# Two-block transformer on one core: the norms' logarithm and exponential from one table set, pair sums on VectorE, low halves by tile, fewer filler matmuls

## The chip, the cores and the metric

The kernel runs on one core of a Trainium2 chip. The metric is the device time of one launch in microseconds, taken as the median over runs. The engines are TensorE (PE), VectorE (DVE), ScalarE (ACT), GpSimd (POOL), and SyncE (SP), which issues the weight transfers.

## The reference: what is computed

Two stacks of two layers each, over 256 tokens of width 1024. In the first, every layer is three half steps, and each ends in the same update: a layer norm of a weighted sum of the input and a gated branch. The result goes, scaled and shifted, into the next matrix product. The second stack, over 272 rows, normalises by the root mean square (RMS) ahead of a mixer with three branches and of a gated convolutional feed-forward.

```python
def layer_norm(x, g, b):
    mu = jnp.mean(xf, axis=-1, keepdims=True)
    var = jnp.mean(jnp.square(xf - mu), axis=-1, keepdims=True)
    return ((xf - mu) * lax.rsqrt(var + LN_EPS)) * g + b
def post_norm_update(x, y, gate, res_w, g, b):
    return layer_norm(DN_ALPHA * x + res_w * gate * y, g, b)
def _rms(x):
    return xf * lax.rsqrt(jnp.mean(xf * xf, axis=-1, keepdims=True) + EPS)
# mixer: retention, hgrn2 and differential attention, each head's output
# through _rms, then a gate, then a product with w_branch
```

There are six layer norms (0 to 5) and five RMS norms of the whole width (0 to 4; the last is the output). The three mixers of each layer have an RMS norm over each head.

## The kernel before

Activations lie feature-major: a tile `k` (0 to 7) holds 128 features on the partitions and the tokens along the free axis, 512 tokens in norms 0 (latent and context rows), 256 in norms 1 to 5, 272 in the RMS norms. Every matrix product is done in three passes on numbers split into a high and a low half: `high*high`, `high*low`, `low*high`. Weights come in chunks of four tiles: SP loads `raw`, ACT casts it to `high` (L2068), DVE subtracts to get `low` (L2291). With `NSLOT` = 4 slots these run up to four chunks ahead of TensorE. The order of work on each engine is the order in which the code of its block issues it; engines meet only in semaphores. A *unit* is 256 output columns: two chunks of four input tiles each (in the steps after a norm), and in each chunk `j` = 0 and 1 pick the output tile, so that every input tile is used in a chunk with `j` = 0 and again with `j` = 1.

A norm is a place where the next product needs the norm's result and TensorE has nothing else to do. For a layer norm the chain is: ones-matmuls sum the rows; DVE centres them in four pairs of tiles (`TC`, L2597); ACT squares each pair (`TQ`, L2233); TensorE sums the eight squared tiles with eight ones-matmuls (L547), two behind each pair; ACT takes the logarithm (L2235) and the exponential (L2238), which is `rdev`, the reciprocal deviation. Then, tile by tile, DVE scales (`scaled`, L2335), ACT adds the shift and casts to the high half (L2082), and DVE subtracts for the low half (`x_low_pair`, L2345). TensorE waits for low halves in pairs of tiles (`s_xl`), in the first unit. The RMS norms do the same with `rms_act` (L1735, L1738) and `rms_dve` (L1749, L1754), the latter in halves of four tiles.

ScalarE keeps one set of function tables at a time. The builder puts an `ACT_TABLE_LOAD` ahead of a function that the loaded set lacks: in every norm one ahead of the logarithm and another ahead of the exponential. The sigmoids need a third set.

`keep_busy(pe, n)` issues `n` matmuls whose result nobody reads (L553), to fill TensorE's time in the chain: three after the row sums, four ahead of the wait for `rdev` and six behind it.

At the end of a mixer of the second stack the heads' outputs are squared, summed on TensorE, and go through logarithm and exponential (`tail_logs`, L711 and L715; `tail_exps`, L724), in two halves, on ScalarE; DVE scales, ACT and DVE split into `OH` and `OL`. Meanwhile TensorE works at the merge gates (`mgate`) from weights split early (`early_split`). Ahead of the `branch` product TensorE waits for a bank that the sigmoid of a merge gate (L2154) must have read; DVE passes that on (L2500). In mixer 1 TensorE also waits, ahead of the merge gates, for the first logarithm (`s_oln`).

## Time and profile before

| | |
|---|---|
| Device time, median of 3 runs | 3049.11 us (3046.49 to 3050.3) |
| Span of the profiled execution, first to last instruction | 3044.0 us |
| TensorE busy with matmuls, fillers among them | 2923.9 us (96%) |
| VectorE busy | 1757.0 us (58%) |
| ScalarE busy | 1380.5 us (45%) |
| Mean granted clock of TensorE, share of full | 0.991 |

The profile gives for its own execution the span; a device time is given for the runs alone, and their median lies 5.1 us above the span, which is what is around it. TensorE's busy time counts fillers too, so 96% overstates what it does for the result. In rows of the timeline a float32 matmul of the ones has two records, so that "x16" is eight matmuls.

### The profile page before, as it was taken

To read this page: it belongs to the slowest core of one execution; us is meant where nothing else is said; L and a number is where in the kernel's file an instruction comes from. 1 tells how busy PE (TensorE), PEld (TensorE's weight loads), DVE (VectorE), ACT (ScalarE), POOL (GpSimd) and SP (SyncE) were. 2 spreads that over 40 slices of the span, in tenths; PEclk is the share of its full clock that TensorE was granted. 3 is DMA by queue.
4 is the path that set the end of the run, shared out by engine and by line. 5 is a ranking of instruction groups with operands and counts; after the bars stand their busy time and mean duration, and the time that the engine had idled before them with its cause. 6 is when DMAs were issued, how large, how long until landed. Compare 5 with 4: busy or idle time off the path is not lost. (4 is left out here: it accounts for less than half of the span.)

```text
span 3044.0 us, 51451 instructions
## 1 busy us (share of the span) xinstructions
PE 2923.9 (96%) x19512; PEld 2567.3 (84%) x19512; DVE 1757.0 (58%) x2624; ACT 1380.5 (45%) x1948; POOL 375.6 (12%) x306
## 2 busy tenths in 40 slices
PE   6999999899999999999899999999999999999998
PEld 3667766677888889888899889799999998988998
DVE  2323224266766657665545865757745577566784
ACT  1222213135655545554453553556644454546663
POOL 2111000123111110111100110101101002020110
PEclk9999999999999999999999999999999999999999
DMA  9886353741565655465435405245545451533563
GB/s 331 281 253 189 114 160 127 194 152 56 165 186 147 193 183 152 147 192 184 133 121 170 146 30 179 84 144 147 170 158 158 142 163 44 156 108 115 156 179 132
DMA packets 586156, 474.80 MB, mean 156 GB/s; under 512 B 28720, under 2 KB 547888, under 8 KB 585664
## 3 DMA queue, kind: packets, MB, share of 16 engines
q1 hardware_dynamic: 584464, 460.44, 49.3%
q0 software_dynamic: 1520, 11.95, 1.3%
q8 instruction: 122, 2.00, 0.3%
q14 instruction: 50, 0.41, 0.0%
HBM read 471.23 MB, written 4.72 MB: 156 GB/s over the span
## 5 line engine op out<-in xcount | busy, mean ns | idle before, releaser
L2291 DVE TENSOR_TENSOR low<-raw,high 128x1024 fp32r<-128x1024 f32 (+1 forms) x744 | 905.6, 1220 | 811.7 <-ACT high L2068 809.3
L2068 ACT CAST high<-raw 128x1024 fp32r<-128x1024 f32 (+1 forms) x744 | 768.3, 1034 | 1001.6 <-PE PS L1980 600.6
L1978 PE MATMUL PS<-NHh,high 128*128 128x272 f32 (+1 forms) x2304 | 669.2, 290 | 14.2 <-DVE NHl L1754 4.7
L1980 PE MATMUL PS<-NHh,low 128*128 128x272 f32 (+1 forms) x2304 | 661.2, 287 | 0.0
L1979 PE MATMUL PS<-NHl,high 128*128 128x272 f32 (+1 forms) x2304 | 660.2, 287 | 0.0
L1978 PEld LDWEIGHTS PS<-NHh,high 128*128 128x128 f32 x2304 | 433.4, 188 | 19.5 <-issue 15.4
L1979 PEld LDWEIGHTS PS<-NHl,high 128*128 128x128 f32 x2304 | 434.0, 188 | 0.8
L1980 PEld LDWEIGHTS PS<-NHh,low 128*128 128x128 f32 x2304 | 433.7, 188 | 0.0
L1976 PE MATMUL PS<-XX,high 128*128 128x512 f32 x966 | 346.8, 398 | 0.0
L1978 PE MATMUL PS<-XX,high 128*128 128x512 f32 (+1 forms) x752 | 273.6, 364 | 3.7 <-DVE XX L2345 2.2
L1975 PE MATMUL PS<-XX,low 128*128 128x256 f32 x966 | 271.2, 281 | 0.3
L1979 PE MATMUL PS<-XX,high 128*128 128x512 f32 (+1 forms) x752 | 266.0, 354 | 0.0
L1980 PE MATMUL PS<-XX,low 128*128 128x512 f32 (+1 forms) x752 | 265.8, 354 | 0.0
L1976 PEld LDWEIGHTS PS<-XX,high 128*128 128x128 f32 x966 | 181.5, 188 | 37.6
L1978 PEld LDWEIGHTS PS<-XX,high 128*128 128x128 f32 x752 | 143.5, 191 | 54.6 <-issue 35.5
L1975 PEld LDWEIGHTS PS<-XX,low 128*128 128x128 f32 x966 | 182.3, 189 | 8.0 <-issue 1.1
L2673 POOL TENSOR_TENSOR GG<-SG,GG 128x256 f32 (+1 forms) x92 | 94.1, 1023 | 729.6 <-ACT GG L2187 639.9
L1980 PEld LDWEIGHTS PS<-XX,low 128*128 128x128 f32 x752 | 143.4, 191 | 20.3
L1979 PEld LDWEIGHTS PS<-XX,high 128*128 128x128 f32 x752 | 143.6, 191 | 17.8
L1976 PE MATMUL PS<-GG,high 128*128 128x512 f32 x420 | 149.4, 398 | 0.0
L1975 PE MATMUL PS<-GG,low 128*128 128x256 f32 x420 | 118.1, 281 | 0.9 <-POOL GG L2673 0.9
L1978 PE MATMUL PS<-OH,high 128*128 128x272 f32 (+1 forms) x384 | 111.7, 291 | 4.6 <-DVEq L2500 4.6
(355 smaller groups left out, 4938.9 us busy)
## 6 DMA issues: line engine op xcount, KB each, us to landing
raw<-w_in_dram SPq DMA_DIRECT2D x416, 256.0 KB, 3.1
raw<-ffn_w_in_dram SPq DMA_DIRECT2D x352, 256.0 KB, 3.4
part<-ada_w_dram SPq DMA_DIRECT2D x184, 256.0 KB, 4.2
raw<-w_ffn_in_dram SPq DMA_DIRECT2D x176, 256.0 KB, 3.2
raw<-ffn_w_out_dram SPq DMA_DIRECT2D x160, 256.0 KB, 3.1
raw<-w_branch_dram SPq DMA_DIRECT2D x96, 256.0 KB, 3.1
raw<-w_ffn_out_dram SPq DMA_DIRECT2D x80, 256.0 KB, 2.9
part_sg<-ada_w_dram SPq DMA_DIRECT2D x48, 256.0 KB, 3.0
```

The lines of the kernel that those rows point to most:

```text
L1975: nc.tensor.matmul(out, wl, xh, start=False, stop=False)
L1976: last = nc.tensor.matmul(two, wh, both, start=False, stop=end)
L1978: nc.tensor.matmul(out, wh, xh, start=begin, stop=False)
L1979: nc.tensor.matmul(out, wh, xl, start=False, stop=False)
L1980: last = nc.tensor.matmul(out, wl, xh, start=False, stop=end)
L2068: nc.scalar.copy(high[:, slot, 0:nk, :], raw[:, slot, 0:nk, :]).then_inc(s_high, 1)
L2291: nc.vector.tensor_tensor(low[:, slot, 0:nk, :], raw[:, slot, 0:nk, :], high[:, slot, 0:nk, :].bitcast(F32), ALU.subtract).then_inc(s_low, 1)
L2673: nc.gpsimd.tensor_tensor(out, x, h.bitcast(F32), ALU.subtract).then_inc(s_hl, 1)
```

## The change

1. **One set.** `log_exp_set()` asks for the set that holds both logarithm and exponential. It is called at the start of every step `res` and `add` (the residual products ahead of the norms), at the start of mixer 0's end, in mixer 1's end behind the early gates, and ahead of mixer 2's small exponential. The sigmoids behind each norm load their own set as before.
2. **Squares in pairs.** For the last two pairs of squared tiles DVE adds the two tiles of the pair (`s_sqp`), and TensorE sums the result with one ones-matmul instead of two: six in place of eight. Only in the layer norms.
3. **Vectors earlier.** The per-feature vectors of a norm (`columns`, `xg`, `xb`) are made in the residual step behind its second unit (`norm_vectors`), no longer between centring and `rdev`.
4. **By tile.** DVE's `scaled` and low-half operations are interleaved, two tiles apart, and TensorE waits tile by tile. In the RMS norms the low halves are made in pairs of tiles in place of fours, and TensorE waits by pairs.
5. **Fewer fillers.** Four and six around the wait for `rdev` become two and three; in the RMS norms five and five become two and four.

```diff
-        def ret_act(act, layer, early_split, early_gate):
+        def ret_act(act, layer, early_split, early_gate, log_exp_set):
+            log_exp_set()
...
             early_gate(1)
+            log_exp_set()
             early_split(1)
...
             dve.wait_ge(s_rrd, m + 1)
-            for hf in range(2):
-                for k in range(4 * hf, 4 * hf + 4):
-                    out = s_rmod if m < 4 else s_modd_final
-                    nc.vector.scalar_tensor_tensor(TN[:, k, :], H[:, k, :], col(name, layer * KT + k),
-                                                   RS[:, 1, 0:T2], ALU.mult, ALU.mult).then_inc(out, 1)
-                if m < 4:
-                    k = slice(4 * hf, 4 * hf + 4)
-                    dve.wait_ge(s_rxh, 4 * m + 2 * hf + 2)
-                    nc.vector.tensor_tensor(NHl[:, k, :], TN[:, k, :], NHh[:, k, :].bitcast(F32),
-                                            ALU.subtract).then_inc(s_rxl, 1)
+            def low_pair(v):
+                k = slice(2 * v, 2 * v + 2)
+                dve.wait_ge(s_rxh, 4 * m + v + 1)
+                nc.vector.tensor_tensor(NHl[:, k, :], TN[:, k, :], NHh[:, k, :].bitcast(F32),
+                                        ALU.subtract).then_inc(s_rxl, 1)
+
+            for k in range(KT):
+                out = s_rmod if m < 4 else s_modd_final
+                nc.vector.scalar_tensor_tensor(TN[:, k, :], H[:, k, :], col(name, layer * KT + k),
+                                               RS[:, 1, 0:T2], ALU.mult, ALU.mult).then_inc(out, 1)
+                if m < 4 and k >= 2 and k % 2 == 0:
+                    low_pair(k // 2 - 1)
+            if m < 4:
...
-                                if name in ("glu", "v", "cgate") and (rolled(s) or not u) and j == 0 and k % 2 == 0:
-                                    pe.wait_ge(s_xl, 4 * norms + (k0 + k) // 2 + 1)
+                                if name in ("glu", "v", "cgate") and (rolled(s) or not u) and j == 0:
+                                    pe.wait_ge(s_xl, KT * norms + k0 + k + 1)
+                                if s.get("after_rms") and (rolled(s) or not u) and j == 0 and k % 2 == 0:
+                                    pe.wait_ge(s_rxl, 4 * (rmss - 1) + (k0 + k) // 2 + 1)
...
-                    for v in range(4):
+                    for v in range(2):
                         pe.wait_ge(s_sq, 4 * norms + v + 1)
-                        last = ones_pair(VAR_BANK, TQ, T, v)
+                        ones_pair(VAR_BANK, TQ, T, v)
+                    for v in (2, 3):
+                        pe.wait_ge(s_sqp, 2 * norms + v - 1)
+                        last = nc.tensor.matmul(PS[:, VAR_BANK, 0:T], ones[:], TQ[:, 2 * v, 0:T], start=False,
+                                                stop=(v == 3))
                     last.then_inc(s_var, 1)
                     norms += 1
-                    keep_busy(pe, 4)
+                    keep_busy(pe, 2)
                     pe.wait_ge(s_rdev, norms)
-                    keep_busy(pe, 6)
+                    keep_busy(pe, 3)
                     if norms == 6:
                         for v in range(4):
                             rms_pe_pair(pe, rmss, v)
                         rmss += 1
-                        keep_busy(pe, 5)
+                        keep_busy(pe, 2)
                         pe.wait_ge(s_rrd, rmss)
-                        keep_busy(pe, 5)
+                        keep_busy(pe, 4)
                 if s.get("rms"):
                     pe.wait_ge(s_free, U_end + 2)
                     keep_busy(pe, 2)
                     rms_pe_pair(pe, rmss, 3)
                     rmss += 1
                     if rmss < 5:
-                        keep_busy(pe, 5)
...
+            def log_exp_set():
+
+                nc.scalar.preload_act_table_set("natural_log_exp_and_others")
...
+                if name in ("res", "add"):
+                    log_exp_set()
...
                     if s.get("at") == 9216 and u == 2:
+                        log_exp_set()
                         lambda_act(act, s["layer"])
...
+            def norm_vectors(m):
+
+                if m < 5:
+                    dve.wait_ge(s_mod, (6 * (m + 1) + 3) // TURN + 1)
+                    columns(m + 1)
+                al = ALPHA if m < 5 else 1.0
+                link(nc.vector.tensor_scalar(sm("xg"), col("ln_g", m * KT, KT), al, None, ALU.mult))
+                link(nc.vector.tensor_scalar(sm("xb"), col("ln_b", m * KT, KT), al, None, ALU.mult))
...
+                    if name == "res" and u == 1:
+                        norm_vectors(norms)
...
+                    for v in (2, 3):
+                        dve.wait_ge(s_sq, 4 * m + v + 1)
+                        nc.vector.tensor_tensor(TQ[:, 2 * v, 0:T], TQ[:, 2 * v, 0:T], TQ[:, 2 * v + 1, 0:T],
+                                                ALU.add).then_inc(s_sqp, 1)
                     if m < 5:
                         dve.wait_ge(s_mod, (6 * (m + 1) + 5) // TURN + 1)
-                        columns(m + 1)
                         gates(m + 1)
-                    al = ALPHA if m < 5 else 1.0
-                    link(nc.vector.tensor_scalar(sm("xg"), col("ln_g", m * KT, KT), al, None, ALU.mult))
-                    link(nc.vector.tensor_scalar(sm("xb"), col("ln_b", m * KT, KT), al, None, ALU.mult))
...
-                        for hf in range(2):
-                            scaled(hf, T)
-                            x_low_pair(m + 1, 2 * hf, T)
-                            x_low_pair(m + 1, 2 * hf + 1, T)
+                        scaled(0, T)
+                        scaled(1, T)
+                        for k in range(KT):
+                            if k + 2 < KT:
```

How the order moves, at three places. The first is ScalarE around norm 1 (`TQ` are squares, `RS` the deviation, `XX` the high halves). Before:

```order
L2068 CAST high<-raw 128x1024 x8
L2233 ACTIVATE TQ<-TC 128x2x256 x4
L2235 ACT_TABLE_LOAD
L2235 ACTIVATE RS<-PS,epsc 128x256
L2238 ACT_TABLE_LOAD
L2238 ACTIVATE RS<-RS 128x256
L2082 ACTIVATE XX<-TQ,small 128x256 x8
```

and now:

```order
L2108 ACT_TABLE_LOAD
L2079 CAST high<-raw 128x1024 x8
L2250 ACTIVATE TQ<-TC 128x2x256 x4
L2252 ACTIVATE RS<-PS,epsc 128x256
L2255 ACTIVATE RS<-RS 128x256
L2093 ACTIVATE XX<-TQ,small 128x256 x8
```

The two loads within the norm are gone, and one stands ahead of the eight casts of the residual step's weights. The second place is VectorE in the same norm (`TC` centred rows, `small` the per-feature vectors, `XX` the low halves). Before:

```order
L2597 SCALAR_TENSOR_TENSOR TC<-PS,X 128x2x256 x4
L2306 TENSOR_SCALAR small<-mod 128x8
L2307 TENSOR_TENSOR small<-small,cols 128x8
L2308 TENSOR_TENSOR small<-small,mod 128x8
L2309 TENSOR_TENSOR small<-small,cols 128x8
L2313 TENSOR_SCALAR small<-mod 128x8
L2604 TENSOR_SCALAR small<-cols 128x8
L2605 TENSOR_SCALAR small<-cols 128x8
L2335 SCALAR_TENSOR_TENSOR TQ<-TC,small,RS 128x256 x4
L2345 SCALAR_TENSOR_TENSOR XX<-TQ,small,XX 128x256 x4
L2335 SCALAR_TENSOR_TENSOR TQ<-TC,small,RS 128x256 x4
L2345 SCALAR_TENSOR_TENSOR XX<-TQ,small,XX 128x256 x4
```

and now:

```order
L2624 SCALAR_TENSOR_TENSOR TC<-PS,X 128x2x256 x4
L2628 TENSOR_TENSOR TQ<-TQ 128x256 x2
L2340 TENSOR_SCALAR small<-mod 128x8
L2361 SCALAR_TENSOR_TENSOR TQ<-TC,small,RS 128x256 x3
L2370 SCALAR_TENSOR_TENSOR XX<-TQ,small,XX 128x256
L2361 SCALAR_TENSOR_TENSOR TQ<-TC,small,RS 128x256
L2370 SCALAR_TENSOR_TENSOR XX<-TQ,small,XX 128x256
L2361 SCALAR_TENSOR_TENSOR TQ<-TC,small,RS 128x256
L2370 SCALAR_TENSOR_TENSOR XX<-TQ,small,XX 128x256
```

Six small operations have left the norm (they stand in the residual step, behind its second unit), two additions of squares have come in, and the groups of four scalings and four low halves have become a run in which they take turns. The third is ScalarE at the end of mixer 1 (`QB` squares of the heads, `MJ` logarithm and exponential, `GR_108` gates). Before:

```order
L2123 ACTIVATE GR_108<-PS 128x544
L2068 CAST high<-raw 128x1024
L1312 ACTIVATE QB<-PS 128x544 x4
L711 ACT_TABLE_LOAD
L711 ACTIVATE MJ<-PS,epsc 128x1088
L2068 CAST high<-raw 128x1024
L711 ACTIVATE MJ<-PS,epsc 128x1088
L724 ACT_TABLE_LOAD
L724 ACTIVATE MJ<-MJ 128x1088 x2
```

and now:

```order
L2137 ACTIVATE GR_108<-PS 128x544
L2108 ACT_TABLE_LOAD
L2079 CAST high<-raw 128x1024
L1315 ACTIVATE QB<-PS 128x544 x4
L712 ACTIVATE MJ<-PS,epsc 128x1088
L2079 CAST high<-raw 128x1024
L712 ACTIVATE MJ<-PS,epsc 128x1088
L725 ACTIVATE MJ<-MJ 128x1088 x2
```

Of the two loads one has gone, and the other stands ahead of the cast and the squares.

## Rows read from the trace of the kernel before

**Rows 1.** page, its first line and busy time of TensorE

```profile
span 3044.0 us, 51451 instructions
...
PE 2923.9 (96%) x19512; PEld 2567.3 (84%) x19512; DVE 1757.0 (58%) x2624; ACT 1380.5 (45%) x1948; POOL 375.6 (12%) x306
```

**Rows 2.** chain of waits, TensorE: who waited for whom, us, times, longest

```profile
PE PS L1978 <- DVEq L2500: 4.6, 2, 2.5
```

**Rows 3.** groups by line, ScalarE: busy us, mean ns | idle before

```profile
L2238 ACT ACT_TABLE_LOAD x6 | 7.7, 1283 | 0.1
...
L1738 ACT ACT_TABLE_LOAD x5 | 6.4, 1283 | 0.1
```

**Rows 4.** timeline of norm 1: start, us, engine, line, operation, count, [idle before <-releaser]

```profile
753.71 2.42 ACT L2233 ACTIVATE TQ<-TC 128x512 f32<-128x512 f32 x4 [1.89 <-DVE TC L2597]
...
754.39 3.72 PE L547 MATMUL PS<-TQ,ones 128*128 128x256 f32 x16 [0.32 <-ACT TQ L2233]
...
758.15 0.47 ACT L2235 ACTIVATE RS<-PS,epsc 128x256 f32<-128x256 f32 x1 [0.72 <-PE PS L547]
...
758.64 1.28 ACT L2238 ACT_TABLE_LOAD   x1
...
759.93 0.42 ACT L2238 ACTIVATE RS<-RS 128x256 f32<-128x256 f32 x1
...
760.40 2.46 PEld L553 LDWEIGHTS PS<-con,ones 128*128 128x128 f32 x12 [0.97 <-ACT RS L2238]
...
760.49 1.67 DVE L2335 SCALAR_TENSOR_TENSOR TQ<-TC,small,RS 128x256 f32<-128x256 f32 x4 [3.73 <-ACT RS L2238]
...
763.10 0.47 PE L1972 MATMUL PS<-XX,high 128*128 128x512 f32 x1
...
765.25 1.67 DVE L2345 SCALAR_TENSOR_TENSOR XX<-TQ,small,XX 128x256 fp32r<-128x256 f32 x4
```

**Rows 5.** timeline, one VectorE addition-sized operation

```profile
775.32 0.43 DVE L2539 TENSOR_TENSOR SG<-SG,GU 128x256 f32<-128x256 f32 x1 [0.50 <-ACT SG L2184]
```

**Rows 6.** timeline of norm 0 (two rows)

```profile
498.33 7.10 PE L547 MATMUL PS<-TQ,ones 128*128 128x512 f32 x16 [1.20 <-ACT TQ L2233]
...
513.23 0.47 PE L1978 MATMUL PS<-XX,high 128*128 128x512 f32 x1 [2.22 <-DVE XX L2345]
```

**Rows 7.** timeline of the second RMS norm

```profile
2059.16 0.65 ACT L1742 CAST NHh<-TN 128x544 fp32r<-128x544 f32 x1 [0.98 <-DVE TN L1749]
...
2058.21 1.74 DVE L1749 SCALAR_TENSOR_TENSOR TN<-H,cols,RS 128x272 f32<-128x272 f32 x4 [3.22 <-ACT RS L1738]
...
2064.32 1.29 DVE L1754 TENSOR_TENSOR NHl<-TN,NHh 128x1088 fp32r<-128x1088 f32 x1 [0.71 <-ACT NHh L1742]
...
2065.75 0.36 PE L1978 MATMUL PS<-NHh,high 128*128 128x272 f32 x1 [0.29 <-DVE NHl L1754]
```

**Rows 8.** timeline, end of mixer 1 of layer 0

```profile
1808.80 1.28 ACT L711 ACT_TABLE_LOAD   x1
...
1811.31 0.39 PE L1978 MATMUL PS<-NHh,high 128*128 128x272 f32 x1 [1.11 <-ACT MJ L711]
...
1813.28 1.28 ACT L724 ACT_TABLE_LOAD   x1
...
1825.77 0.57 PE L1978 MATMUL PS<-OH,high 128*128 128x272 f32 x1 [2.10 <-DVEq L2500]
```

**Rows 9.** windows: busy us of each engine, then clock, DMA share, GB/s

```profile
510.00:513.00 3.00, 1.01 (x5) 0.56 (x3) 3.00 (x9) 2.46 (x7) 0.00 (x0) 1.00 0.00 0
...
1471.60:1475.00 3.40, 3.38 (x8) 2.54 (x9) 0.00 (x0) 2.89 (x4) 0.00 (x0) 0.50 0.00 0
...
1475.00:1478.40 3.40, 3.40 (x11) 2.64 (x10) 0.00 (x0) 0.00 (x0) 0.00 (x0) 0.64 0.00 0
...
1825.80:1828.00 2.20, 2.20 (x10) 2.20 (x11) 1.50 (x2) 2.20 (x4) 0.00 (x0) 0.50 0.69 236
...
1828.00:1831.00 3.00, 3.00 (x22) 3.00 (x22) 2.09 (x2) 1.29 (x2) 0.00 (x0) 0.83 0.52 163
```

More of the change, by code:

```diff
@@ L1288, in level_exps, with hg_act @@
             nc.scalar.activation(er, er, ACT.Exp).then_inc(s_ha, 1)
-        def hg_act(act, layer, early_split, early_gate, early_logits):
+        def hg_act(act, layer, early_split, early_gate, log_exp_set, early_logits):
             t, d, a, p = HT * layer, HDV * layer, HAC * layer, HPO * layer
@@ L2083, in x_high_pairs @@
                                                     bias=sm("ab", c)[:, k:k + 1])
-                    if k % 2:
-                        last.then_inc(s_xh, 1)
+                    last.then_inc(s_xh, 1)
             def residual_rows(m, T):
@@ L2263, in _ @@
                                                           lambda u: early_sigmoid(u, steps[n_step + 1]),
-                                                          *([lambda: early_logits(steps[n_step + 1])]
-                                                            if s["mixer"] == 1 else []))
+                                                          *(([log_exp_set], [log_exp_set,
+                                                                             lambda: early_logits(steps[n_step + 1])],
+                                                             [])[s["mixer"]]))
                 if name == "branch" and s["n"] == 2:
```

53 lines of the change are left out of this document (27 added, 26 removed).

## The prediction, made before the run

> **What bounds the kernel now.** The page gives a span of 3044.0 us with TensorE busy for 96% of it [rows 1]. Fillers count as busy, so the places where TensorE does nothing for the result have to be found in the timeline, at each norm. In norm 1 [rows 4] the four pairs of tiles are squared from 753.71 to 756.13; TensorE sums them from 754.39 for 3.72 us without a gap behind its start, so its eight matmuls and not ScalarE end that stage. Then everything is one chain: logarithm at 758.15, a table load at 758.64, exponential at 759.93, VectorE's scaling at 760.49, and TensorE takes up the product at 763.10. The six fillers (2.86 us from 760.40) are about as long as the stop behind the exponential, so they fill it and lengthen it by 0.1 us at most. Such a stop comes 11 times (six layer norms, five RMS norms), and whatever shortens its chain shortens the span by as much, provided that TensorE is not held by the fillers. The groups by line say that the second load stands in each: 6 and 5 times 1283 ns with nearly no idle time ahead [rows 3]. The chain of waits then shows one more place: twice, 4.6 us in all, TensorE waits for VectorE's release of a bank ahead of a branch product [rows 2], and its timeline [rows 8] shows two table loads in the ScalarE work that leads there.
>
> **The change, part by part.**
>
> *Loads.* From the load's start to the exponential's is 1.29 us in norm 1 [rows 4]; the chain has nothing beside it there. 11 x 1.29 = **14.2 us**. The first load of each norm (ahead of the logarithm) lies behind the squares while TensorE still sums, so removing it gives nothing. The load now at the start of `res` and `add` steps lands on ScalarE, busy 45% of the span [rows 1], with weights split up to four chunks ahead: nothing; uncovered it would be 1.28 each.
>
> The Trainium skill ("ScalarE: Activation LUTs", What ACT_TABLE_LOAD costs) puts about 1.38 us of drain on top of the load, 2.66 us for a switch. The trace doesn't show that: the logarithm ends at 758.62, the load begins at 758.64, the exponential 1.29 us behind it [rows 4]. By the page the sum would be some 15 us larger.
>
> *Squares in pairs.* Eight matmuls take 3.72 us in norm 1, 0.465 each, and 7.10 in norm 0, 0.89 each [rows 4, 6]. Two fewer: 1.8 us in norm 0, 0.93 in norms 1 to 5, 4.65 together. Now VectorE must have the last sum in time: square at 756.13, an addition of 128x256 takes 0.43 [rows 5], so 756.6, and TensorE comes to its sixth matmul at 754.39 + 5 x 0.465 = 756.7. It fits with 0.1 to spare; without it I would lose some tenths a norm. I take **6.4 us**. The vectors that leave the norm ended long ahead of the exponential, so their move gives nothing there, but it makes room for the additions. In the residual step six to ten small operations of VectorE (58% busy) now stand ahead of a low half; I take nothing, with 1 us for each of six norms at the far end.
>
> *Waits by tile, layer norms.* VectorE does 16 operations from 760.49 to 766.92 [rows 4], 0.40 apart. Before, tiles 0 and 1 are there at +2.4 and TensorE starts at 763.10, +2.6. Now tile 0 comes after four operations, +1.7, then one more tile per 0.8 us, and tile 7 at the same +6.4. But a tile's three passes need 0.36 us, so TensorE waits between tiles, ends the first chunk's second output tile at about +5.9 and the second chunk at +8.7, just where it ends before (the last low half, then 2 x 0.36 and 4 x 0.36). An earlier start is spent waiting: **0**, between -0.8 (the whole earlier start) and +0.2 a norm.
>
> *RMS norms.* Before [rows 7]: scalings from 2058.21, the second half's low operation ends at 2065.61, TensorE's second chunk starts at 2065.75, +7.5. It needs 3.05 us: +10.6. Now pairs: scalings at 0.43, a cast of 0.65 and a low operation of half of 1.29 plus fixed cost, say 0.7; in turn they give pairs at +2.4, 4.3, 6.1 and 8.0. TensorE then has one pair with `j` = 0 (0.76) and the whole of `j` = 1 (1.52) left: +10.3. Saves 0.3, four times: **1.2 us**.
>
> *Fillers.* They hide nothing for the result, but if they were left at four and six, they would now be late: the six summing matmuls end at 757.2, two fillers of 0.48 end at 758.1, and `rdev` comes at about 758.2; four would hold TensorE until 759.1. Behind it three end at +1.4, ahead of tile 0 at +1.7. So the reduction itself is worth nothing beyond letting the other terms through. Idle stretches grow by less than 1 us a norm.
>
> *End of mixer 1.* Here [rows 8] ScalarE goes from load (1808.80) to logarithm, cast, second logarithm, load (1813.28), exponential, without idle time; VectorE and ScalarE take turns until the gate's sigmoid frees the bank at 1825.77. Both loads leave this chain: the first moves into idle time ahead of the squares (the cast behind it is 1.3 later, with a slack of 1.9 us to the next square). 2 x 1.28 less a tenth for a sum that TensorE ends at 1810.2: 2.5 us. TensorE's two gaps there, 1.11 and 2.10 us, hold 3.2, so it can follow, with 0.7 us of gap left. Two layers: **5.0 us**. In mixers 0 and 2 TensorE shows no such wait: nothing.
>
> *Clock.* Behind that 2.10 us gap the granted clock is 0.50 for 2.2 us and 0.83 for 3 us [rows 9], that is 1.2 GHz of 2.4 for a time. The lost work is 2.2 x 0.5 + 3 x 0.17 = 1.6 us, and the same in the other layer, where the gap is 2.5 (4.6 less 2.1, rows 2). With the gap at 0.7 to 1.1 I expect the clock to stay up, as it did behind the 1.11 gap: **3.3 us**.
>
> Sum: 14.2 + 6.4 + 0 + 1.2 + 5.0 + 3.3 = 30.1 us. The profiled span would be 3014, and with 5.1 around it, or from the median of the runs, 3049.1 - 30.1 = **3019 us**, -1.0%. A measurement of this kernel tells about 0.2% (6 us) from no change.
>
> **Rivals.** (a) *The clock takes back a part.* Norm 0 is where fewer fillers can hurt: TensorE waited 2.22 us there at full clock [rows 6, 9]; now it has 1.9 us of gap and then 0.7 busy in every 1.6 us, since its tiles are twice as wide. The price of a fall: from 1471.60 to 1478.40, behind 4.39 us of idle time in norm 5, the clock was 0.50 and 0.64, a loss of 3.4 x 0.5 + 3.4 x 0.36 = 2.9 us [rows 9]. Three such stretches, and the 3.3 us not gained, give 3049 - 30 + 8.7 + 3.3 = 3031. The Trainium skill ("TensorE: Matmul & The Clock Gate", Part 1) says that the half rate is the resting state and that only activity lifts it, which speaks for this rival and against the fillers' removal; the trace agrees behind 4.39 and 2.10 us, and doesn't behind 2.22 and 1.11. Chance 0.22, 3027 to 3040.
>
> (b) *Slower.* The same mechanism at every stop: ten norms ahead of a product, each falling to half rate. At 2.9 us each that is 29, against 26.8 gained without the clock term: 3051. Slower by 0.2% needs 3.3 us a stop or more. Gaps after the change are about 1 us or less in nine of the ten, so I give it 0.02 for beyond +0.2%, 0.02 for ending near the old time.
>
> (c) *A switch costs more than its load*, as the page has it: then 11 x 1.38 = 15 us more, 3004. What speaks against it is the 0.02 us between logarithm and load. Chance 0.04.
>
> (d) *The stops are not the bound*, since weights land too late behind them and TensorE then waits for SP's transfers. The transfers' share is 0.00 in norm 0's stop [rows 9]: all slots are full, so they start from TensorE's progress and shift with it. Were it so, only the last norm and mixer 1's end would gain, some 7 us: 3042. Chance 0.04. That the loads stay in place is excluded by the order shown above.
>
> **How the numbers follow.** The forecast case, 0.66, spans 3010 to 3027: down by half-clock stretches elsewhere in the mixers that may or may not come back with other timing, and by 0.8 us a norm from tile waits; up by the vectors' 6 us or a late addition. Taking in most of (a) the range is 3009 to 3032. Faster 0.95 (forecast, c, nearly all of a, d), same 0.03, slower 0.02.
>
> **What would show it.** Right: no ACT_TABLE_LOAD between logarithm and exponential in 11 norms; in norm 1 from the first square to the logarithm 3.5 us in place of 4.44, and from it to VectorE's scaling 1.05 in place of 2.34; TensorE's first unit behind a layer norm ending 8.7 us after the first scaling as before; the gap ahead of mixer 1's branch product at about 1 us, with the clock at 1.00 behind it. Wrong: the clock under 1.00 behind norms 0 to 4, or a summing matmul that waits for VectorE's addition by more than 0.3 us, or TensorE's waits for weights appearing in a norm's shadow.

## The result, and the profile after

The changed kernel takes 3014.26 us (median of 4 runs, 3006.44 to 3015.33), the kernel before 3047.8 us (4 runs, 3044.93 to 3050.3). The ratio on record is 0.9893, 95% interval 0.9878 to 0.9907. By the medians it is 33.5 us less, where 30.1 were forecast. (Ratios here are taken against the kernel before as it ran beside each kernel, and differ from the quotient of the medians by up to 0.002.) The profiled execution took 3014.72 us with a span of 3012.9.

The page of the changed kernel, its first line and the busy times, answers to [rows 1]:

```profile
span 3012.9 us, 51229 instructions
...
PE 2898.0 (96%) x19396; PEld 2540.7 (84%) x19396; DVE 1765.8 (59%) x2644; ACT 1356.7 (45%) x1928; POOL 375.3 (12%) x306
```

TensorE is 26 us less busy, mostly for the 58 fillers and summing matmuls that it no longer does, and still at 96%. The share tells nothing of where the time came from. For that, norm 1 in the timeline of the changed kernel (start, us, engine, line, operation, count, idle time before):

```profile
752.98 2.42 ACT L2250 ACTIVATE TQ<-TC 128x512 f32<-128x512 f32 x4 [1.89 <-DVE TC L2624]
...
753.67 1.99 PE L548 MATMUL PS<-TQ,ones 128*128 128x256 f32 x8 [0.32 <-ACT TQ L2250]
754.84 0.42 DVE L2628 TENSOR_TENSOR TQ<-TQ 128x256 f32<-128x256 f32 x1
...
755.44 0.43 DVE L2628 TENSOR_TENSOR TQ<-TQ 128x256 f32<-128x256 f32 x1 [0.17 <-ACT TQ L2250]
755.50 1.12 PE L2034 MATMUL PS<-TQ,ones 128*128 128x256 f32 x4
...
756.65 0.47 ACT L2252 ACTIVATE RS<-PS,epsc 128x256 f32<-128x256 f32 x1 [1.25 <-PE PS L2034]
757.16 0.42 ACT L2255 ACTIVATE RS<-RS 128x256 f32<-128x256 f32 x1
...
757.72 1.27 DVE L2361 SCALAR_TENSOR_TENSOR TQ<-TC,small,RS 128x256 f32<-128x256 f32 x3 [1.77 <-ACT RS L2255]
...
759.53 0.47 PE L1979 MATMUL PS<-XX,high 128*128 128x512 f32 x1 [0.34 <-DVE XX L2370]
...
766.45 0.40 PE L1979 MATMUL PS<-XX,high 128*128 128x512 f32 x1
```

The last row is the first matmul of the second unit (L1979 is issued for a unit's first tile alone, once for each `j`). The same matmul in the kernel before:

```profile
769.16 0.40 PE L1972 MATMUL PS<-XX,high 128*128 128x512 f32 x1
```

Against [rows 4]: no table load stands between logarithm and exponential. From the logarithm to VectorE's scaling it is 757.72 - 756.65 = 1.07 us, before 2.34 (forecast 1.05). From the first square to the logarithm it is 3.67 us, before 4.44 (forecast 3.5); in norm 0 the same stretch went from 8.34 to 6.62 us. The product starts 1.81 us behind the scaling (before 2.61), but TensorE is through with the first unit at the same distance as before: 766.45 - 757.72 = 8.73 us, before 769.16 - 760.49 = 8.67 (forecast 8.7). The earlier start is spent in waits between tiles. The copy that takes the unit out, 11.54 us behind the scaling (769.26) and before 11.56 (772.05), can't show this: it stands behind eight ScalarE operations (L2103, from 765.31 for 4.05 us).

The groups by line for ScalarE; the loads are now 38 in all (before 58). The largest group holds those called ahead. Its idle time before is 0.3 us, as little as that of the loads in the chain ([rows 3]: 0.1): a load follows the instruction ahead of it at once in either place, so this column doesn't tell whether it is hidden. The segments below do.

```profile
L2108 ACT ACT_TABLE_LOAD x16 | 20.5, 1283 | 0.3
```

The end of mixer 1 in layer 0, which answers to [rows 8]; the last square before was at 1808.15, the branch product at 1825.77:

```profile
1796.02 0.62 ACT L1315 ACTIVATE QB<-PS 128x544 f32<-128x544 f32 x1 [3.11 <-DVE EX L1502]
1796.54 1.16 ACT L712 ACTIVATE MJ<-PS,epsc 128x1088 f32<-128x1088 f32 x1
...
1798.52 1.19 ACT L712 ACTIVATE MJ<-PS,epsc 128x1088 f32<-128x1088 f32 x1
1799.59 2.12 ACT L725 ACTIVATE MJ<-MJ 128x1088 f32<-128x1088 f32 x2
...
1809.93 0.62 ACT L2168 ACTIVATE GR<-PS 128x544 f32<-128x544 f32 x1
...
1810.78 0.36 PE L1985 MATMUL PS<-OH,high 128*128 128x272 f32 x1 [0.61 <-DVEq L2525]
```

From the last square to the product 14.76 us in place of 17.62, and the gap is 0.61 us in place of 2.10. The chain of waits has for both layers, against 4.6 us in [rows 2],

```profile
PE PS L1985 <- DVEq L2525: 1.9, 2, 1.2
```

Behind it the clock stays up; windows of both layers (busy us of PE, PEld, DVE, ACT, POOL, then clock, DMA share, GB/s), which answer to the last two of [rows 9]:

```profile
1810.80:1813.00 2.20, 2.20 (x18) 2.20 (x18) 1.48 (x2) 2.20 (x4) 0.00 (x0) 1.00 0.73 238
1813.00:1816.00 3.00, 3.00 (x26) 3.00 (x25) 2.88 (x3) 1.95 (x2) 0.00 (x0) 1.00 0.65 214
2583.60:2586.00 2.40, 2.40 (x20) 2.40 (x21) 1.73 (x2) 2.40 (x4) 0.00 (x0) 1.00 0.69 219
```

**A ruler that is finer than the total.** Runs of one kernel scatter by 5 to 26 us, mostly 10 to 20, more than most terms of the forecast. But the starts of the 11 logarithms of the norms cut a trace into segments, and a segment of the layer norms or R1-R2 without a stretch at half clock (a *fall*) repeats to 0.1 us. The last segment, R3-R4, doesn't: see the end. From norm 1 to norm 2 it is 954.04 - 756.65 = 197.39 us in the changed kernel and 957.52 - 758.15 = 199.37 before. The table has these differences for all kernels of this study, one profiled execution each (N: layer norm, R: RMS norm; from N1 to N4 and from R1 to R2 the segments hold no fall unless marked *; the others can hold some).

```
kernel                     N1-N2   N2-N3   N3-N4   N5-R0   R0-R1   R1-R2   R2-R3
before                    199.37  199.39  105.80   16.34  577.49  209.68  568.76
before, again             199.38  199.40  105.81   14.95  576.09  209.66  568.58
before, gap filled        199.39  199.37  105.79   15.16  576.26  209.67  568.72
before + loads ahead      198.10  198.12  104.60   14.67  572.62  208.40  560.05
after                     197.39  197.37  103.88   15.17  571.09  208.08  559.65
after, again              197.38  197.43  103.88   14.68  576.59  208.08  559.90
after, old fillers        197.40  197.39  103.90   13.60  572.21  208.09  560.00
after, no fillers         198.58* 198.25* 104.59*  15.13  573.51  209.15* 563.10
after, no pair sums       198.15  198.21  104.64   14.63  576.58  208.09  559.71
after, old order          197.35  197.36  103.77   14.90  573.50  209.29* 562.62
after, tail loads kept    197.46  197.44  103.88   13.76  575.59  208.08  565.82
after, norm 5 filled      197.38  197.38  103.89   12.17  575.05  208.09  563.77
after, all gaps filled    197.44  197.44  103.87   12.30  569.81  208.09  562.42
after, filled in layer 0  197.44  197.38  103.88   12.30  571.27  208.09  560.87
```

### The profile page after: what moved, and what is told of

It reads as the page before. It is cut to its first block and busy times, and to the rows that moved or that the text cites. A ratio compares the mean times of both kernels' runs of the same rounds, so it can differ in the third digit from the quotient of the medians.

```text
span 3012.9 us, 51229 instructions
## 1 busy us (share of the span) xinstructions
PE 2898.0 (96%) x19396; PEld 2540.7 (84%) x19396; DVE 1765.8 (59%) x2644; ACT 1356.7 (45%) x1928; POOL 375.3 (12%) x306
## 3 DMA queue, kind: packets, MB, share of 16 engines
q8 instruction: 121, 1.98, 0.3%
## 5 line engine op out<-in xcount | busy, mean ns | idle before, releaser
L1985 PE MATMUL PS<-GG,high 128*128 128x512 f32 (+1 forms) x324 | 113.6, 351 | 0.0
```

What stands on the lines that cost most here:

```text
L1985: nc.tensor.matmul(out, wh, xh, start=begin, stop=False)
```

## The experiments

Theory: each stop is a chain whose every link counts one for one, the clock gives back something at mixer 1, and the fillers hide nothing. Rivals: the fillers' number is what gains; the clock takes back a part; the pairs or the order are absorbed.

**1. The loads alone** (the kernel before with the set loaded ahead).

```
+            def log_exp_set():
+                nc.scalar.preload_act_table_set("natural_log_exp_and_others")
...
+            log_exp_set()          # at the start of res, add and mixer 0's end, in mixer 1 behind early_gate(1)
```

> The kernel before with the table set of logarithm and exponential loaded ahead at the change's places, and nothing else of the change: eight summing matmuls, the old order of scaling and low halves, and the old fillers. The forecast's terms that are in it: 11 loads of 1.29 (14.2 us), the end of mixer 1 (5.0 us), the clock behind it (3.3 us): 22.5 us, 3025 us. If the old fillers hold TensorE behind the shorter chain (they end about 4.8 us behind the sums, the first low pair now comes at about 3.5 us, so they could hold it by 1.3 us at each of 11 stops), only 8 to 9 us are left of it: 3039 us. The forecast says that this is absorbed, since TensorE waits again for later tiles.

Measured: 3025.2 us (6 runs, 3019.57 to 3030.31), ratio 0.9936 (0.9920 to 0.9951). The segments fall by 1.27, 1.27, 1.20 and, from R1 to R2, 1.28 us: one load per stop. The old fillers don't hold it back. By the medians this one part is two thirds of the gain.

**2. The old numbers of fillers** in the changed kernel.

```
-                    keep_busy(pe, 2)
+                    keep_busy(pe, 4)
                     pe.wait_ge(s_rdev, norms)
-                    keep_busy(pe, 3)
+                    keep_busy(pe, 6)
...
```

> The changed kernel with the old numbers of fillers (four and six in the layer norms, five and five in the RMS norms). In norms 1 to 5 the product would start at about 761.4 in place of 759.5, where the last tile's low half comes at 764.1, so the first unit ends about 0.8 us later: 5 x 0.8 = 4 us, nothing in norm 0 and the RMS norms: 3018 us. If the smaller number of fillers is what the gain comes from, all 11 stops grow by 1.1 to 1.9 us: 3027 to 3035 us. If fillers keep the clock up, it is faster than the changed kernel.

Measured: 3012.82 us (6 runs, 3008.48 to 3026.12), ratio 0.9905 (0.9886 to 0.9923): no difference to the changed kernel. Both expectations for the stops fell, the 0.8 us a norm too. In its trace, norm 1 has

```profile
749.38 4.48 PE L554 MATMUL PS<-con,ones 128*128 128x256 f32 x20
...
753.51 0.58 PE L1979 MATMUL PS<-XX,high 128*128 128x512 f32 x1
...
759.38 0.39 PE L1979 MATMUL PS<-XX,high 128*128 128x512 f32 x1
```

All ten fillers run without a break, and the product starts 2.86 us behind the scaling (750.65), 1.05 us later than in the changed kernel. The second unit begins 8.73 us behind the scaling (759.38), as with few fillers (8.73). TensorE catches up what it starts late, because it waits less for later tiles; I had put the product's start 0.8 us later than it comes. The reduction of fillers is worth nothing in the chain. Whether more fillers keep the clock up more often isn't decided: the medians are 1.4 us apart.

**3. No fillers** from the last sum of a norm to the product.

```
                     norms += 1
-                    keep_busy(pe, 2)
                     pe.wait_ge(s_rdev, norms)
-                    keep_busy(pe, 3)
...
```

> The changed kernel with no fillers between the last summing matmul of a norm and the product behind it (those ahead of the sums stay). By the forecast's chain alone nothing moves: 3014 us. By its rival on the clock TensorE is now idle for 2.3 to 3.7 us at 11 stops, and each fall costs 1.6 to 2.9 us: up to 18 to 32 us, 3032 to 3046 us. I expect falls at some stops, 5 to 15 us: 3019 to 3029 us.

Measured: 3023.54 us (6 runs, 3016.58 to 3027.6), ratio 0.9926 (0.9910 to 0.9941): about 9 us given back. Norm 2 in its trace, the product's start and then windows around it:

```profile
958.69 0.47 PE L1979 MATMUL PS<-XX,high 128*128 128x512 f32 x1 [2.92 <-DVE XX L2364]
```

```profile
957.00:960.00 3.00, 1.20 (x4) 0.75 (x4) 3.00 (x8) 2.05 (x5) 0.00 (x0) 0.91 0.00 0
960.00:963.00 3.00, 3.00 (x10) 2.30 (x10) 3.00 (x9) 1.80 (x4) 0.00 (x0) 0.52 0.00 0
963.00:966.00 3.00, 3.00 (x19) 2.67 (x18) 3.00 (x4) 1.78 (x3) 0.00 (x0) 1.00 0.01 3
```

The clock is at its lower level (0.52 is 1.2 GHz for nearly all of that window) behind every one of the norms that a product follows, layer and RMS, for a lost work (half of TensorE's busy time at half clock) of some 1.5 to 2.9 us each, where the changed kernel has none from norm 1 to 4. So the forecast's rival on the clock describes something real, and a few fillers are what keeps it away. A fall costs less than its lost work: segments N1-N2 and N2-N3 are only 1.19 and 0.88 us longer, since TensorE waits for tiles in that stretch anyway.

**4. No sums in pairs**: eight matmuls again, no additions.

```
-                    for v in (2, 3):
-                        dve.wait_ge(s_sq, 4 * m + v + 1)
-                        nc.vector.tensor_tensor(TQ[:, 2 * v, 0:T], TQ[:, 2 * v, 0:T], TQ[:, 2 * v + 1, 0:T],
-                                                ALU.add).then_inc(s_sqp, 1)
```

> The changed kernel with eight summing matmuls in each layer norm and no additions on VectorE. By the forecast 6.4 us slower; by what the trace of the changed kernel shows in norms 0 and 1 (1.72 and 0.77 us shorter), 1.72 + 5 x 0.77 = 5.6 us: 3020 us. If the two fillers and the wait for the reciprocal root absorb it, 3014 us.

Measured: 3019.2 us (6 runs, 3014.8 to 3022.82), ratio 0.9915 (0.9901 to 0.9930). The segments are 0.76, 0.84 and 0.76 us longer. In this execution the clock also fell behind norm 0 (within 510 to 516 us, behind the same 1.93 us gap as in the changed kernel), as it did in experiment 7, and not in the two traces of the changed kernel. So 0.8 us a norm; with the 1.72 us that norm 0 shows in the trace of the changed kernel 5.6 to 5.7 us.

**5. The old order** of scaling and low halves, and TensorE's waits by pairs and halves.

```
-                        scaled(0, T)
-                        scaled(1, T)
-                        for k in range(KT):
-                            if k + 2 < KT:
-                                scaled(k + 2, T)
-                            x_low_tile(m + 1, k, T)
+                        for hf in range(2):
+                            for k in range(4 * hf, 4 * hf + 4):
+                                scaled(k, T)
+                            for k in range(4 * hf, 4 * hf + 4):
+                                x_low_tile(m + 1, k, T)
```

> The changed kernel with VectorE's old order in the norms (four tiles scaled, then their four low halves; RMS norms: the low half of four tiles in one instruction) and TensorE's waits by pairs and by halves as before. By the forecast nothing in the layer norms and 0.3 us in each of four RMS norms, 1.2 us: 3015.5 us. If an earlier first product is worth its 0.8 us at each layer norm, 4 to 5 us more: 3020 us.

Measured: 3018.45 us (6 runs, 3012.44 to 3022.56), ratio 0.9915 (0.9896 to 0.9933), which doesn't tell it from the changed kernel. The segments do: in the layer norms 1 to 4 the order is worth nothing (197.35, 197.36, 103.77 us). But R1-R2 is 1.2 us longer, not 0.3. In the second RMS norm of this trace:

```profile
2042.45 0.36 PE L1983 MATMUL PS<-NHh,high 128*128 128x272 f32 x1 [1.88 <-DVE NHl L1752]
```

```profile
2040.00:2043.00 3.00, 1.12 (x7) 0.75 (x6) 2.29 (x4) 0.80 (x2) 0.00 (x0) 1.00 0.00 1
2043.00:2046.00 3.00, 3.00 (x16) 3.00 (x15) 2.25 (x4) 1.29 (x2) 0.00 (x0) 0.53 0.00 0
```

By halves and with few fillers the gap is 1.88 us and the clock falls behind it. It does so in four of its norms: 0, and RMS norms 0, 1 and 3. With the old fillers (experiment 1, old order too) R1-R2 has no fall and is 208.40, 0.32 us above the changed kernel. The order alone gives that 0.32. Beyond it, it shortens the gap: with the new order and the same few fillers it is 0.48 us in the RMS norms, and behind RMS norms 1 to 3 no fall stands in five traces (15 places), against two of three here. At norm 0 the new order's gap is still 1.93 us, and there experiment 4 has a fall too.

**6. Mixer 1's loads back in its chain** (the changed kernel without the early load there).

```
             early_gate(1)
-            log_exp_set()
             early_split(1)
```

> The changed kernel without the early load at mixer 1's end, so that both table loads stand in the chain there again, in two layers. The chain was 2.86 us shorter from the last square to the branch product, so 5.7 us slower, and by the forecast the gap ahead of the branch product is back at 2 us and the clock falls behind it, 3.3 us more: 3023 us. Without the clock 3020 us.

Measured: 3026.06 us (12 runs, 3018.14 to 3044.04), ratio 0.9953 (0.9932 to 0.9973), against 0.9893 for the changed kernel: more than expected, and a total too scattered to size this part: four of the twelve runs took 3041 to 3044 us, the other eight 3018 to 3030, and why is open. The profiled span, 3018.9 us, is nearer. The chain is exact: from the last square to the gate's sigmoid it is 16.77 us in both layers in all four traces in which the loads stand there, and 13.91 in all others. The gap ahead of the branch product is back:

```profile
1809.03 0.56 PE L1984 MATMUL PS<-OH,high 128*128 128x272 f32 x1 [2.10 <-DVEq L2524]
```

```profile
1809.00:1812.00 3.00, 2.97 (x13) 3.00 (x14) 2.23 (x2) 3.00 (x4) 0.00 (x0) 0.50 0.55 175
1812.00:1815.00 3.00, 3.00 (x24) 3.00 (x23) 1.39 (x3) 1.19 (x2) 0.00 (x0) 0.93 0.85 276
```

and the clock falls behind it, in both layers. The chain is 5.7 us longer, as expected. The clock's part is less sure: from the sigmoid to the next norm it is 1.5 us (layer 0) and 3.2 us (layer 1, with a second fall at 2727) longer than in the first trace of the changed kernel, but in layer 0 it is 4.0 us shorter than in that kernel's second trace.

**7. The gap alone** (the kernel before with three fillers in it).

```
+                if name == "mgate" and s["n"] == 1:
+                    pe.wait_ge(s_oln, half_first(s["layer"], 1) + 2)
+                    keep_busy(pe, 3, 6)
```

> The kernel before with three fillers (1.4 us) in the gap ahead of mixer 1's branch product, in two layers, and nothing of the change. It tests the clock term alone: the gap of 2.1 and 2.5 us becomes 0.7 and 1.1. By the forecast the clock stays up and 3.3 us are gained: 3044.5 us. If it is not the gap that brings the clock down, no change: 3047.8 us.

Measured: 3041.78 us (12 runs, 3035.68 to 3048.41), the kernel before beside it 3045.94; ratio 0.9996 (0.9982 to 1.0009). The total doesn't show 3 us, and doesn't exclude it: the interval reaches from 5.5 us less to 2.7 more and holds both expectations. In the trace the gap is 0.81 us in layer 0 and 1.22 in layer 1, and the clock is 1.00 behind it in both, which fits that the fall comes from the gap; one trace doesn't prove it, since experiment 11 has the full gap in layer 0 without a fall. And R2-R3 is 568.72 us, as before: a stretch at half clock of 4.7 us of lost work now stands at 2739 to 2754. A fall that is prevented in one place was not a gain in the segment.

**8. Norm 5 filled**: ten fillers in the wait for the first RMS norm's squares.

```
                     if norms == 6:
+                        keep_busy(pe, 10)
                         for v in range(4):
```

> The changed kernel with ten fillers (4.8 us) in the 5.7 us in which TensorE waits for the squares of the first RMS norm, behind norm 5. The clock was 0.50 behind it for 6 us, a loss of 3.0 us. If the gap is the cause, 3.0 us faster than the changed kernel: 3011 us; else 3014 us.

Measured: 3014.76 us (6 runs, 3010.54 to 3019.0), ratio 0.9904 (0.9886 to 0.9921). Windows of the changed kernel there, and then of this one:

```profile
1458.00:1461.00 3.00, 0.08 (x1) 0.08 (x1) 0.00 (x0) 2.97 (x7) 0.00 (x0) 0.87 0.02 5
1461.00:1464.00 3.00, 3.00 (x7) 2.30 (x8) 0.00 (x0) 1.50 (x3) 0.00 (x0) 0.50 0.00 0
1464.00:1467.00 3.00, 3.00 (x9) 2.19 (x8) 0.00 (x0) 0.00 (x0) 0.00 (x0) 0.50 0.00 0
```

```profile
1458.00:1461.00 3.00, 1.97 (x9) 1.66 (x10) 0.00 (x0) 2.58 (x5) 0.00 (x0) 1.00 0.00 0
1461.00:1464.00 3.00, 2.83 (x13) 2.06 (x12) 0.02 (x1) 0.92 (x2) 0.00 (x0) 1.00 0.00 0
```

N5-R0 is 12.17 us in place of 15.17: the expected 3.0 (against the second trace of the changed kernel, 14.68, it is 2.5). The total doesn't show it; in this execution R0-R1 is 4.0 us longer than in the first trace, with falls at 1916 and 1946, and R2-R3 4.1 us, with falls at 2700 and 2724.

**9. All gaps filled**: norm 5, mixer 1's two first gaps (the wait for a free bank moves behind the first of them), the old numbers in the norms.

```
+            keep_busy(pe, 2, 5)            # ahead of mixer 1's scores
...
+                if n == 0:
+                    keep_busy(pe, 6, 5)    # ahead of its first level
```

> The changed kernel with fillers wherever TensorE is idle for over 1.4 us ahead of a stretch at half clock and a bank is free: ten behind norm 5, two ahead of mixer 1's scores, six ahead of its first level, and in the norms the old numbers (four and six, five and five), which the second experiment showed to cost nothing. The norm's own segments should stay at 197.4 us. Behind norm 5 3.0 us gained, in mixer 1 the falls behind its two gaps gone, 1.5 us in each layer up to 5 us in layer 1: 3014 less 3 less 3 to 7, 3004 to 3008 us. If each fall only moves to the next gap, as the total of the kernel with norm 5 filled suggests, 3013 us.

Measured: 3011.9 us (4 runs, 3008.34 to 3013.49), ratio 0.9889 (0.9868 to 0.9910). R0-R1 is 569.81 us without a fall. R2-R3 is 562.42, 2.8 us longer than in the changed kernel, though the long stretch at half clock at 2496 to 2508 is gone: two falls at 2694 and 2718 cost more. The long stretch cost little: from R2's logarithm to the last square of mixer 1 it is 321.71 us with it (changed kernel, 2247.06 to 2568.77) and 321.46 without (here, 2240.82 to 2562.28). The changed kernel has there

```profile
2502.00:2505.00 3.00, 3.00 (x15) 2.33 (x13) 3.00 (x1) 0.00 (x0) 2.64 (x1) 0.50 0.00 0
```

VectorE is busy without a break, and TensorE at half rate only spends time that it would wait for VectorE. At full clock (experiment 8) it stands still instead:

```profile
2505.00:2508.00 3.00, 0.33 (x3) 0.12 (x2) 3.00 (x5) 1.81 (x2) 2.97 (x1) 1.00 0.00 0
```

**10 and 11. Both kernels once more**, unchanged, for second traces.

> The changed kernel once more, unchanged, for a second trace and runs on this chip. If the stretches at half clock are fixed by the kernel, they stand at the same places as in its first trace (576, 726, 1458, 1734, 2496 us); if they differ from one execution to the next, some have moved, and the span differs by 1.5 to 3 us for each, while the segments between the logarithms without such a stretch (197.4 us between norms 1 and 2) repeat within 0.1 us.

> The kernel before once more, unchanged, for a second trace. Its segment between norms 1 and 2 should be 199.4 us again. The gaps at norm 5 (4.4 us) should bring a stretch at half clock again; those at 1824 and 2607 us, ahead of mixer 1's branch product, too if the forecast's clock term is a property of that gap; those at 552 and 2715 us may be gone or elsewhere.

Measured: after 3017.35 us (6 runs, 3012.86 to 3029.0), ratio 0.9912 (0.9892 to 0.9933); before 3047.42 us (12 runs, 3039.85 to 3050.77), ratio 1.0007 (0.9998 to 1.0017). The segments N1-N2 to N3-N4 and R1-R2 repeat within 0.06 us. The falls are not fixed by the kernel: the changed kernel's at 726 is gone, others stand at 544, 1920, 1950 and 1960; those at 576, 1458, 1734 and about 2500 are there again. The three new ones in mixer 2 of layer 0 make R0-R1 576.59 us in place of 571.09, and then the whole gain of this segment over the kernel before (577.49 and 576.09) is gone:

```profile
1920.00:1923.00 3.00, 3.00 (x21) 2.64 (x14) 2.24 (x11) 1.16 (x5) 0.43 (x1) 0.51 0.23 79
1950.00:1953.00 3.00, 2.24 (x11) 2.01 (x12) 2.82 (x16) 1.92 (x9) 0.00 (x0) 0.54 0.51 175
```

Ahead of mixer 1's branch product the kernel before shows the same gaps (4.6 us, two, longest 2.5), but in layer 0 no fall this time:

```profile
1821.48 0.36 PE L1978 MATMUL PS<-OH,high 128*128 128x272 f32 x1 [2.10 <-DVEq L2500]
```

```profile
1820.00:1823.00 3.00, 1.52 (x12) 1.55 (x13) 1.35 (x2) 2.99 (x4) 0.00 (x0) 1.00 0.43 141
1823.00:1826.00 3.00, 3.00 (x26) 3.00 (x26) 2.88 (x4) 2.65 (x4) 0.00 (x0) 1.00 0.56 192
```

**12. Filled in layer 0 only.**

```
+                if n == 0 and layer == 0:
+                    keep_busy(pe, 6, 5)
```

> The kernel with all gaps filled, less the fillers in mixer 1 of layer 1, where the 5 us at half clock lie behind VectorE, which is busy without a break there: ten fillers behind norm 5, two and six in mixer 1 of layer 0, old numbers in the norms. The segment behind norm 5 should be 12.3 us, RMS norm 0 to 1 about 569.8 us as with all gaps filled, and RMS norm 2 to 3 back at 559.7 us in place of 562.4, if the two falls at 2700 and 2725 us come from the missing long stretch at half clock ahead of them: 3009 us. If those two falls are chance, 562 to 563 us again, and 3012 us.

Measured: 3006.74 us (5 runs, 2998.03 to 3014.78), ratio 0.9875 (0.9855 to 0.9894). N5-R0 is 12.30 us as expected, R0-R1 571.27 with one fall, R2-R3 560.87 with no fall at 2700: between the two expectations. The long stretch near 2500 is missing here too (a short fall stands at 2506), so the falls at 2700 and 2725 don't come from its absence alone. It is the best median of all, 7.5 us under the changed kernel's, but its interval (0.9855 to 0.9894) overlaps that one's (0.9878 to 0.9907). It is faster than the kernel before for certain; that it beats the changed kernel is shown for the stretch behind norm 5 (2.4 to 2.9 us), not for the whole.

## Why the prediction was right, point by point

*Loads, 14.2 us:* right. 1.20 to 1.31 us in each of the six segments that hold no fall (experiment 1; the two that the table lacks are N4-N5, 199.41 to 198.10, and R3-R4, 198.85 to 197.57), 11 of them 13 to 14 us. Rival (c) is out: taking the load away shortens the stop by the load's own 1.28 us and no more. By the Trainium skill ("ScalarE: Activation LUTs", What ACT_TABLE_LOAD costs) a drain of some 1.38 us would have gone with each, an estimated 15 us more in all; the traces don't agree. Rival (d) is out too: the stops are what bounds, or the segments wouldn't have shortened by what was taken out of them.

*Squares in pairs, 6.4 us:* the mechanism was right, the size some 0.7 us too high. Norm 0 gave 1.72 of the 1.8 forecast, norms 1 to 5 0.8 in place of 0.93. Norm 1's records say why. Within the row of eight they start 0.216 us apart, two to a matmul, so two matmuls fewer are 0.86 us; 0.465 was the mean over the row, with its longer first record and its end. And the last sum starts its second record 0.09 us late, behind an addition that ends at 755.86: 0.86 - 0.09 = 0.77. The margin of 0.1 us that I counted on wasn't quite there, but the wait stays far under the 0.3 us named as a sign of being wrong.

*Vectors earlier, 0:* not undone by itself. N1-N2 fell by 1.98 us in all, the loads by experiment 1 give 1.27 of it and the pairs by experiment 4 0.76, so no cost of the moved operations can be seen there, let alone the 1 us a norm at the far end.

*Waits by tile in the layer norms, 0:* right, and for the reason given (experiment 5: 197.35 against 197.39).

*RMS norms, 1.2 us:* right where a segment without falls can tell, 0.32 us in R1-R2. R3-R4 doesn't show it: experiment 1 has 197.57 us with the old order, the changed kernel 196.72 and 197.59. What the forecast lacked is that the old order with the new, small number of fillers brings the clock down in four norms (experiment 5); the parts of the change are not independent here.

*Fillers, nothing in the chain:* right (experiment 2). The step beside it, that four and six would be "late", is half right: the product starts 1.05 us later with them and loses nothing by it.

*End of mixer 1, 5.0 us:* 2 x 2.86 = 5.7 us. I had taken a tenth off for a sum that TensorE ends late; instead the chain gave 0.3 us more than its two loads (2.57) in each layer. The rows of layer 0 show where: the kernel before has, beside those of [rows 8],

```profile
1808.15 0.62 ACT L1312 ACTIVATE QB<-PS 128x544 f32<-128x544 f32 x1 [3.11 <-DVE EX L1499]
...
1812.09 1.17 ACT L711 ACTIVATE MJ<-PS,epsc 128x1088 f32<-128x1088 f32 x1
...
1814.58 2.12 ACT L724 ACTIVATE MJ<-MJ 128x1088 f32<-128x1088 f32 x2
```

From the last square to the first logarithm it went from 1.94 to 0.52 us, from the second logarithm to the exponential from 2.49 to 1.07: 1.42 us for each load. Without a load between them the second activation starts 0.10 to 0.12 us before the first one's end (1796.54 against 1796.02 + 0.62; 1799.59 against 1798.52 + 1.19); the load starts behind it. In norm 1 the exponential needs the logarithm's result and starts 0.04 us behind its end, so there nothing comes on top of the 1.28.

*Clock behind it, 3.3 us:* the link between gap and fall is shown, the gain isn't. With the gap at 2.1 and 2.5 us the clock fell in five of six cases (both layers of before and of experiment 6, one of before again), with it at 0.6 to 1.3 us in none of 22 (eleven traces without the loads or with the gap filled, two layers). But what the span gets of it is settled further on. From that sigmoid to the next norm's logarithm (us, and the falls in between):

```
kernel                    layer 0      layer 1
before                    231.03, 1    228.62, 3
before, again             229.59, 0    228.45, 3
before, gap filled        230.67, 1    229.02, 2
after                     229.05, 0    224.03, 0
after, again              234.53, 3    224.14, 0
```

One fall behind the gap costs 1.4 us in layer 0 (231.03 against 229.59), not far from the 1.6 of the forecast. In layer 1 the stretch went down by 4.3 to 4.6 us in place of 1.7, because two falls in mixer 2 (at 2715 and 2745 in both traces of before) are missing in both traces of the changed kernel. In layer 0 it went down by 2.0 us from the first trace to the first, and up by 4.9 from the second to the second, with three falls in mixer 2 that neither trace of before has; experiments 4 and 8 have falls there too. So the forecast's two places gave 6.6 us in the first pair of traces and took 0.6 in the second. What decides on the falls in mixer 2 is open: the two gaps of TensorE there are 1.97 to 1.98 and 1.31 us long in both layers and in all four of these traces, with and without falls behind them, and in layer 1 experiments 3, 5, 8 and 9 have falls again. Counted afterwards, the five traces with the load ahead in mixer 1 that have the long stretch near 2500 have none behind it, and of the five without it four have; experiment 12 is the fifth, so this is no rule.

*The sum.* Chain by these measurements: 11 x 1.28 + 5.7 + 4 x 0.32 + 5.7 = 26.8 us, forecast 26.8 without the clock. That these agree to 0.1 is luck in part: the pairs were 0.7 too high and mixer 1 0.7 too low. The medians leave 6.7 us beside the chain in the first set of runs and 3.3 in the second (3047.42 - 3017.35 = 30.1), for the clock and the start together; 3.3 were forecast for the clock, and no run shows that it is those. The traces speak against a fixed clock term. From norm 0's logarithm to the last one the chain terms are 23.8 us (ten loads, five pairs of 0.8, the RMS norms, mixer 1). The first two traces differ by 31.3 us there (2527.77 less 2496.45), the second two by 20.4 (2520.84 less 2500.49): 7.5 us on top, and 3.4 us taken back. So the chain is what this study confirms; the 3.3 us is smaller than what one execution of a kernel differs from the next, and that the total came out within 5 us of 3019 owes something to chance. The start, up to norm 0's logarithm, adds its own scatter: that logarithm comes at 505.5, 506.5 and 509.2 us in the traces of the kernel before and its filled form, at 507.0 and 508.6 in the changed kernel, though the pair sums take 1.7 us out ahead of it, and at 503.5 to 507.7 in its variants. The 5.1 us that I put around the span are 1.8 in the profiled runs here (3014.72 less 3012.9, 3039.85 less 3038.0), so the first profiled execution's own time was not comparable to its span in that way; taken from the median of the runs, the forecast didn't depend on it.

*Rival (a), the clock takes back a part:* did not come true at norm 0 nor at norms 1 to 4, which run at 1.00 in both traces of the changed kernel, but experiment 3 shows that it was near: without the last five fillers it does, and in experiment 4 it did at norm 0, the place that the forecast named. Its price of 2.9 us a fall was too high for these stops: 0.7 to 1.2 us of the segment. Where the clock did take back, in the second trace, was mixer 2 of layer 0, a place that neither the forecast nor the rival named.

## What to carry to other kernels

Follow each stop of the bounding engine as a chain; every instruction of another engine in it counts at its full length, and a table load there is best called where that engine is idle, in a set that holds both functions. Fillers gain nothing by their number, but some must stay. At the norms of this kernel no fall stands behind a gap of 1.54 us or less, while 1.88 us had one in three of four RMS norms and 1.93 us in one of five traces at norm 0: keep the gap ahead of a product well below these, and change order and fillers together. It is no limit for other places: in mixer 2, where TensorE is partly idle around it, a gap of 1.31 us had a fall behind it in some traces (2747 in the kernel before, 1950 in the changed kernel's second) and none in others. Where runs scatter more than an edit is worth, measure it between fixed landmarks of the trace, choose a landmark on the engine that bounds, and compare two traces of the same kernel before a stretch at half clock is blamed on an edit or a clock gain is credited to it.

## What the runs showed of the hardware

The clock's falls are partly chance: the same kernel with the same 2.10 us gap fell in one execution (windows of [rows 9]) and not in another (experiment 11). The Trainium skill ("TensorE: Matmul & The Clock Gate", Part 1) says that the monitor behind the clock runs freely and isn't reset by the kernel's start. The two traces of each kernel, with falls in different places, fit that and don't prove it. The lost work of a fall is mostly 1.4 to 1.7 us, else 2.5 to 3.4 us or some 5 us. And lost work isn't lost time: 5 us of it beside a VectorE that was busy without a break cost 0.25 us (321.71 against 321.46), 1.7 us in layer norms 1 to 3, with waits between tiles, cost 0.7 to 1.2 (experiment 3), and 3.0 us behind norm 5 cost 3.0.

A table load cost its own 1.28 us where the next activation waited for the one before it anyway, and 1.42 us where the two would have overlapped.

From R3 to R4 the changed kernel took 196.72 us in one trace and 197.59 in the other, both at full clock. The other kernels with the loads ahead and no fall there took one of these two values, within 0.03 us; the three traces of the kernel before and its filled form took 198.85. What switches between the two is open, and it is a warning that a segment at full clock can still have two lengths, 0.9 us apart.
